# A decoder layer on one core: the last two output-projection pairs, two norms and the first feed-forward round by token halves, in one list schedule

## The reference

```
h = hybrid_mixer(rmsnorm(x, mix_pre_norm[i]), ...)      # ends with: mixed @ w_out, 2048 -> 1024
x = x + rmsnorm(h, mix_post_norm[i])
h = swiglu(rmsnorm(x, ffn2_pre_norm[i]), ffn2_w_gate[i], ffn2_w_up[i], ffn2_w_down[i])
...
def rmsnorm(x, g):
    y = xf * lax.rsqrt(jnp.mean(xf * xf, axis=-1, keepdims=True) + NORM_EPS)
    return (y * g.astype(jnp.float32)).astype(x.dtype)
def swiglu(x, w_gate, w_up, w_down):
    return (jax.nn.silu(x @ w_gate) * (x @ w_up)) @ w_down
```

## Time and profile before

| | |
|---|---|
| median of 3 runs | 2328.41 us (2323.27 to 2330.6) |
| the profiled execution | 2320.75 us, span of its trace 2319.1 us |
| TensorE busy | 2232.7 us, 96% of the span |
| VectorE busy | 1748.3 us, 75% |
| ScalarE busy | 858.4 us, 37% |
| share of TensorE in the chain that ended last | 88% |

### The profile page before, as it was taken

How to read it: one execution, slowest core, us unless ns; L and a number is a source line. 1 busy time by engine, 2 the same in 40 slices (tenths; PEclk the granted TensorE clock), 3 DMA queues, 4 the chain that set the end, 5 groups by cost and what they waited for, 6 DMA issues and landing times.

```text
span 2319.1 us, 29269 instructions
## 1 busy us (share of the span) xinstructions
PE 2232.7 (96%) x10358; PEld 1824.7 (79%) x10358; DVE 1748.3 (75%) x2661; ACT 858.4 (37%) x1357; POOL 206.3 (9%) x181
## 2 busy tenths in 40 slices
PE   7999999999999989999999998998999999999996
PEld 6888888888878767778787677786888888888885
DVE  7877777777768888887776976878787777777766
ACT  6322222222344556665532644214522222222222
POOL 0000000000000333432100316100000000000000
PEclk9999999999999999999999999998999999999998
DMA  4111111111332001002031224114111111111123
GB/s 158 50 55 46 50 54 54 54 54 54 118 111 91 10 19 37 28 28 73 12 108 46 91 91 172 54 43 176 37 64 46 54 54 54 54 54 54 46 100 109
DMA packets 52041, 154.62 MB, mean 67 GB/s; under 512 B 5872, under 2 KB 7920, under 8 KB 49776
## 3 DMA queue, kind: packets, MB, share of 16 engines
q1 hardware_dynamic: 51952, 153.46, 19.5%
HBM read 132.14 MB, written 21.30 MB: 66 GB/s over the span
## 4 chain that ended last, share of the span: by engine, by line
PE 88%; DVE 7%; ACT 2%; issue 2%; DMA 1%; SPq 0%; DVEq 0%; ACTq 0%
PE psum L456 10%; PE psum L455 10%; PE psum L454 10%; PE psum L593 8%; PE psum L594 8%; PE psum L595 8%; PE psum L1640 3%; PE psum L1642 3%; PE psum L1641 3%; PE psum L1786 2%; PE psum L541 1%; PE psum L543 1%; PE psum L542 1%; PE psum L1797 1%; PE psum L1163 1%
## 5 line engine op out<-in xcount | busy, mean ns | idle before, releaser
L1009 DVE TENSOR_TENSOR acc<-psum,acc 128x512 f32<-128x512 f32 x288 | 197.9, 691 | 160.9 <-PE psum L595 158.1
L593 PE MATMUL psum<-act_hi,tile_hi 128*128 128x512 f32 x672 | 261.5, 389 | 0.0
L594 PE MATMUL psum<-act_lo,tile_hi 128*128 128x512 f32 x672 | 261.4, 389 | 0.0
L595 PE MATMUL psum<-act_hi,tile_lo 128*128 128x512 f32 x672 | 261.4, 389 | 0.0
L708 ACT CAST t_hi<-t_raw 128x512 fp32r<-128x512 f32 x144 | 89.6, 622 | 309.9 <-DVE t_raw L869 296.5
L593 PEld LDWEIGHTS psum<-act_hi,tile_hi 128*128 128x128 f32 x672 | 126.1, 188 | 26.2
L595 PEld LDWEIGHTS psum<-act_hi,tile_lo 128*128 128x128 f32 x672 | 126.1, 188 | 26.2
L594 PEld LDWEIGHTS psum<-act_lo,tile_hi 128*128 128x128 f32 x672 | 126.1, 188 | 26.1
L730 ACT ACTIVATE sum<-sum 128x512 f32<-128x512 f32 x72 | 45.6, 633 | 247.6 <-DVE sum L963 152.8
L1640 PE MATMUL psum<-norm_hi,tile_hi 128*128 128x512 f32 x320 | 129.7, 405 | 6.2 <-DVE z_scaled L2047 4.3
L1956 DVE TENSOR_TENSOR probs_t_lo<-psum,probs_t_hi 128x512 fp32r<-128x512 f32 x144 | 96.6, 686 | 47.7 <-ACT probs_t_hi L1874 47.2
(11 more groups left out here) (377 smaller groups left out, 5618.4 us busy)
## 6 DMA issues: line engine op xcount, KB each, us to landing
tile_lo_raw<-in_d SPq DMA_DIRECT2D x40, 512.0 KB, 4.3
gate_raw<-in_gu SPq DMA_DIRECT2D x36, 512.0 KB, 3.8
up_raw<-in_gu SPq DMA_DIRECT2D x72, 256.0 KB, 3.6
raw_tile<-in_w_att SPq DMA_DIRECT2D x28, 512.0 KB, 3.6
gate_up_lo_raw<-in_gu SPq DMA_DIRECT2D x8, 1024.0 KB, 5.2
cum_rows<-cum_scratch SPq DMA_DIRECT2D x8, 1024.0 KB, 4.5
raw_tile<-in_w_out SPq DMA_DIRECT2D x16, 512.0 KB, 3.6
acc<-in_x SPq DMA_DIRECT2D x8, 512.0 KB, 10.7
```

Source lines behind the costliest of these rows:

```text
L593: pe.matmul(o, w_h[:, s, d, :], a_h[:, s, x], start=(s == 0), stop=False)
L594: pe.matmul(o, w_h[:, s, d, :], a_l[:, s, x], start=False, stop=False)
L595: mm = pe.matmul(o, w_l[:, s, d, :], a_h[:, s, x], start=False, stop=(s == 1))
L1009: v.tensor_tensor(x, banks(4 + d % 4), x, ALU.add).then_inc(sem(p + "_acc"), 1)
```

## The change

The last two pairs of the output projection (6 and 7), the post norm of the mixer, the pre norm of the second feed-forward block and that block's first round with its down projection leave their written order and become steps of one plan (`turn_plan`), at the same half-width steps as `t1` and `t3`, and `t2` becomes a half-turn.

- The outputs come in another order: half 0 of pair 6, half 0 of pair 7, then half 1 of both (`OUT_ORDER`). TensorE has outputs, rounds and down outputs in one line "main".
- The post norm is done for each half by itself, and so is the pre norm. The square sums of the pre norm are groups of 4 columns, 16 of them (`cols_of`), in bank 5.
- Scale, residual, high part, square and low part work on half tiles: 16 of each instead of 8. The residual comes in as 16 loads of a half tile, 8 for each half, each into its own place; 16 stores instead of 8.
- In the first round half 0 of both weight tiles comes first (`round 0` is units 0 and 1, 12 matmuls a tile), then half 1 of the first, then half 1 of the second. The down projection's outputs go to other banks (`TURN_DOWN`).
- Pair 7's second weight tile has a raw buffer of its own. The gate/up weights are loaded when pair 7's operands are made, the down weights after the last output. The odd pairs' buffers, the even pairs' weights, the first pair's, and the squares' move to other addresses.
- Ahead of the plan, `out_pe`, `out_act` and `out_dve` end with pair 5, pair 6's operands still made within pair 5. Behind it nothing changes.

The diff, cut to its core. The placing of the buffers:

```diff
         wl = at("tile_lo", 164, [P, 2, KT, P], FR)
-        xs = at("x_stream", 172, [P, 2, S])
+        x_half = [at("x_first_half", 206.75, [P, KT, HALF]), at("x_second_half", 96, [P, KT, HALF])]
+        sq_half = [at("x_squares", 196, [P, 4, HALF]), at("x_squares_next", 172, [P, 4, HALF])]
         sq = at("squares", 180, [P, 2, S])
-        diag = at("rstd_diagonal", 180, [P, CH, P])
-        sqa = at("result_squares", 172, [P, 4, HALF])
+        diag = {"t": at("rstd_diagonal", 180, [P, CH, P]), "g": at("gate_diagonal", 56, [P, CH, P])}
+        sqa = at("result_squares", 112, [P, 4, HALF])
+        raww_last = at("raw_tile_last", 120, [P, KT, P])
         gul_raw = at("gate_up_lo_raw", 136, [P, 2, 2, KT, P])
         wl_raw = at("tile_lo_raw", 164, [P, 2, KT, P])
...
-        out_first = (at("tile_hi_first", 172, [P, 2, KT, P], FR), at("tile_lo_first", 180, [P, 2, KT, P], FR), acth, actl)
-        out_slots = [(wh, wl, acth, actl),
-                     (at("tile_hi_odd", 14, [P, 2, KT, P], FR), at("tile_lo_odd", 22, [P, 2, KT, P], FR),
-                      at("act_hi_odd", 30, [P, 2, S], FR), at("act_lo_odd", 38, [P, 2, S], FR))]
+        out_first = (at("tile_hi_first", 196, [P, 2, KT, P], FR), at("tile_lo_first", 206.75, [P, 2, KT, P], FR), acth, actl)
+        out_slots = [(at("tile_hi_even", 14, [P, 2, KT, P], FR), at("tile_lo_even", 22, [P, 2, KT, P], FR), acth, actl),
+                     (wh, wl, at("act_hi_odd", 172, [P, 2, S], FR), at("act_lo_odd", 180, [P, 2, S], FR))]
 
         psum = ctx.enter_context(nc.psum_tensor("psum", [P, 8, 512], F32))
 
```

The plan, without the sums for the seven-product loop (`planned_sum`, `operand_sum` and their casts, ranks 6 and 7):

```diff
+        OUT_PAIRS = MIX_T // 2
+        OUT_ORDER = [(i, h, d) for h in range(NH2) for i in (OUT_PAIRS - 2, OUT_PAIRS - 1) for d in range(KT)]
+        OUT_DONE = 16 * (OUT_PAIRS - 2)
+        FREE = OUT_DONE + OUT_ORDER.index((OUT_PAIRS - 2, 1, KT - 1)) + 1
+        TURN_BANKS = (0, 2, 6, 0)
+        TURN_DOWN = (4, 5, 2, 3), (4, 5, 6, 7)
+
+        def turn_plan():
+            plan = Plan()
+            add = plan.add
+            last = OUT_PAIRS - 1
+            for n in (2 * last, 2 * last + 1):
+                add("SP", "out_w", ("out_w_in", n), 0.0)
+                add("ACT", "out_w", ("out_w_hi", n), 1.05, ("out_w_in", n))
+                add("DVE", "out_w", ("out_w_lo", n), 1.22, ("out_w_hi", n))
+                add("ACT", "out_w", ("out_a_hi", n), 1.05)
+                add("DVE", "out_w", ("out_a_lo", n), 1.22, ("out_a_hi", n))
+            ready = [("out_w_lo", 2 * last + 1), ("out_a_lo", 2 * last + 1)]
+            for n, u in enumerate(OUT_ORDER):
+                add("PE", "main", ("out", *u), 1.36, ("out_acc", *OUT_ORDER[n - 4]) if n > 3 else None,
+                    *(ready if u[0] == last else ()))
+                add("DVE", "out_acc", ("out_acc", *u), 0.69, ("out", *u))
+            free = ("out", last - 1, 1, KT - 1)
+            whole = ("out_acc", *OUT_ORDER[-1])
+            rings = [(h, d) for h in range(NH2) for d in range(1, KT)]
+            for h in range(NH2):
+                for d in range(KT):
+                    r = rings.index((h, d)) if d else 0
+                    add("ACT", "a_sq", ("a_sq", "t2", h, d), 0.63, ("out_acc", last, h, d),
+                        ("a_sum", "t2", *rings[r - 4]) if r > 3 else None)
+                    if d:
+                        add("DVE", "a_sum", ("a_sum", "t2", h, d), 0.69, ("a_sq", "t2", h, d),
+                            ("a_sum", "t2", h, d - 1) if d > 1 else ("a_sq", "t2", h, 0))
+                rstd_steps(add, f"t2_post{h}", ("a_sum", "t2", h, KT - 1))
+            for n in range(2):
+                add("SP", "gu_in", ("gu_in", n), 6.0, ready[1])
+                add("ACT", "gu", ("gu_hi", n), 2.0, ("gu_in", n))
+                add("DVE", "gu", ("gu_lo", n), 2.3, ("gu_hi", n))
+            for s in range(2):
+                add("SP", "d_in", ("d_in", s), 4.0, ("out", *OUT_ORDER[-1]))
+                add("ACT", "d", ("d_hi", s), 1.05, ("d_in", s))
+                add("DVE", "d", ("d_lo", s), 1.22, ("d_hi", s))
+            for h in range(NH2):
+                for k in range(KT):
+                    add("SP", "x_in", ("x_in", "t2", h, k), 3.0, free if h else None)
+                    add("DVE", "scale", ("scale", "t2", h, k), 0.69, ("rb", f"t2_post{h}"))
+                    add("DVE", "resid", ("resid", "t2", h, k), 0.69, ("scale", "t2", h, k), ("x_in", "t2", h, k))
+                    add("SP", "x_out", ("x_out", "t2", h, k), 3.0, ("resid", "t2", h, k))
+                    add("ACT", "hi", ("hi", "t2", h, k), 0.63, ("resid", "t2", h, k), free if k > 2 else None)
+                    add("DVE", "lo", ("lo", "t2", h, k), 0.69, ("hi", "t2", h, k))
+                    add("ACT", "sq", ("sq", "t2", h, k), 0.63, ("resid", "t2", h, k), ("cols_of", h, k - 4) if k > 3 else None)
+                    add("PE", "cols_of", ("cols_of", h, k), 0.85, ("sq", "t2", h, k),
+                        (("rms", "t2_pre0") if h else whole) if k == 0 else None)
+                e = f"t2_pre{h}"
+                add("ACT", "rstd", ("rms", e), 0.3, ("cols_of", h, KT - 1))
+                add("DVE", "rstd", ("rc", e), 0.9, ("rms", e))
+                add("PE", "rstd", ("rows", e), 1.0, ("rc", e))
+                add("ACT", "rstd", ("rb", e), 0.63, ("rows", e))
+            begin = {0: [("gu_lo", 1), ("rb", "t2_post0")], 2: [("rb", "t2_post1"), whole], 3: [("gate", 0), ("up", 0)]}
+            for v in (0, 2, 3):
+                for k in range(KT):
+                    add("PE", "main", ("round", v, k), 1.36 if v else 2.72, ("lo", "t2", v // 2, k), *(begin[v] if k == 0 else ()))
+            for v in range(4):
+                done = ("round", v if v > 1 else 0, KT - 1)
+                add("DVE", "gate", ("gate", v), 0.69, done, ("silu", v - 1) if v else None, ("rb", f"t2_pre{v // 2}"))
+                add("ACT", "silu", ("silu", v), 0.63, ("gate", v), ("prod", v - 1) if v else None)
+                add("DVE", "up", ("up", v), 0.69, done, ("act_lo", v - 1) if v else None, ("rb", f"t2_pre{v // 2}"))
+                add("DVE", "prod", ("prod", v), 0.69, ("silu", v), ("up", v))
+                add("ACT", "act_hi", ("act_hi", v), 0.58, ("prod", v), ("resid", "t2", 1, KT - 1))
+                add("DVE", "act_lo", ("act_lo", v), 0.69, ("act_hi", v))
+            for h in range(NH2):
+                for d in range(KT):
+                    add("PE", "main", ("down", h, d), 1.36, ("act_lo", 2 * h + 1), ("d_lo", 1),
+                        ("rb", "t2_pre1"), ("down_copy", (8 * h + d - 4) // 8, (d - 4) % 8) if 8 * h + d > 3 else None)
+                    add("DVE", "down_copy", ("down_copy", h, d), 0.69, ("down", h, d), ("planned_sum", 16), ("x_out", "t2", 1, KT - 1))
...
+            rank = dict(RSTD_RANK)
+            rank |= {("DVE", "out_acc"): 1, ("DVE", "a_sum"): 2, ("DVE", "lo"): 2, ("DVE", "resid"): 3, ("DVE", "scale"): 4,
+                     ("ACT", "a_sq"): 1, ("ACT", "hi"): 2, ("ACT", "sq"): 3, ("DVE", "out_w"): 0, ("ACT", "out_w"): 0,
+                     ("PE", "main"): 1, ("PE", "cols_of"): 0, ("DVE", "gate"): 1, ("DVE", "up"): 1, ("DVE", "prod"): 1, ("DVE", "act_lo"): 1,
+                     ("DVE", "down_copy"): 1, ("ACT", "silu"): 1, ("ACT", "act_hi"): 1, ("ACT", "d"): 6, ("ACT", "s"): 6,
+                     ("ACT", "t_hi"): 7, ("DVE", "sums"): 6, ("DVE", "t_sum"): 6, ("DVE", "t_lo"): 7}
+            return plan.order(rank)
+
+        TURN = turn_plan()
+
+        TURN_RSTD = {"t2_post0": (3, 2), "t2_post1": (7, 6), "t2_pre0": (5, 4), "t2_pre1": (5, 4)}
+
```

TensorE's steps and SyncE's; the steps of ScalarE and VectorE hold the same instructions as before at half width, with the waits that the plan lists:

```diff
+            def round_step(v, k):
+                if k == 0 and v == 0:
+                    wait(pe, p + "_gu_lo", 2)
+                    pe.wait_ge(sem("rstd_rb"), RSTD["t2_post0"])
+                elif k == 0 and v == 2:
+                    pe.wait_ge(sem("rstd_rb"), RSTD["t2_post1"])
+                elif k == 0:
+                    wait(pe, p + "_gate", 1)
+                    wait(pe, p + "_up", 1)
+                h = v // 2
+                pe.wait_ge(sem("half_lo"), past_half("t2", h, KT) + k + 1)
+                for u in (0, 1) if v == 0 else (v,):
+                    for m in range(2):
+                        mm = pair(TURN_BANKS[u] + m, u % 2, m, k, h)
+                if k == KT - 1:
+                    mm.then_inc(sem(p + "_gu_mm"), 2 if v == 0 else 1)
+
...
+        def turn_pe(pe, step, e):
+            if step == "out":
+                i, h, d = e
+                n = OUT_DONE + OUT_ORDER.index((i, h, d))
+                w_h, w_l, a_h, a_l = out_slot(i)
+                wait(pe, "wo_d_lo", 2 * i + 2)
+                wait(pe, "wo_act_lo", 2 * i + 2)
+                wait(pe, "wo_acc", n - 3)
+                o, x = banks(4 + d % 4), half(h)
+                for s in range(2):
+                    pe.matmul(o, w_h[:, s, d, :], a_h[:, s, x], start=(s == 0), stop=False)
+                    pe.matmul(o, w_h[:, s, d, :], a_l[:, s, x], start=False, stop=False)
```

(32 more changed lines are left out.)

550 lines of the change are left out of this document (347 added, 203 removed).

## The result

The kernel after takes 2310.03 us (median; 2306.84 to 2316.57 over 4 runs), the kernel before 2327.64 us beside it (2323.27 to 2330.6 over 4 runs). The ratio is 0.9933, 95% interval 0.9914 to 0.9952: faster by 0.67%, 15.6 us (the medians themselves are 17.6 apart). The forecast was 2315.9, a gain of 12.5.

The account below looks back on a forecast made before the run. TensorE was taken as the bound; the 146.7 us stretch becomes 130.0 of work plus 4.2 of waits. The gain, 13.5 + 4.4 - 1.1 - 0.1 - 4.2 = 12.5, gives 2315.9 us; range 2312.9 to 2318.9, over all cases 2310 to 2325.

Parts of the forecast that it names:

- TensorE sets the end, time won ahead of the loop arrives whole: Whole kernel: TensorE, busy 96% of the span, bounds it; time won before the steady loop at 1690.1 us arrives whole.
- Removed 17.2 - 3.7 = 13.5: Post norm after the last output: of a 17.2 us gap only 3.7 us of TensorE helper matmuls stay, saving 13.5.
- Price of the order 1.2: Pair 6's outputs: pair 7's operands, needed earlier, delay accumulations; TensorE stalls 1.2 us, bounds 0 and 3.
- Square sums 16 x 0.98, rows 1.8: Pre norm: 16 column groups at 0.98 us, 15.7 against 14.6; rows as two half ones, 1.8 against 1.7.
- Waits in a list order 4.2: Changed stretch: TensorE idles 4.2 us, as in the earlier half-turn, the 1.2 us stall included; bounds 1.2 and 9.
- Slow clock 4.4 taken as gone: Changed stretch: 3.6 us of slow-clock matmuls and 0.8 us unexplained disappear; bounds -4.4 to 0.
- VectorE 118 to 121: Changed stretch: VectorE's busy time rises from 116.6 us to 118 to 121 with more, half-width instructions.
- The half-0 root within 6 us of half 1: Post norm, a sign to show in the profile: the half-0 root comes within 6 us after half 1 begins.
- Granted clock 1.0 in all of it: From pair 6's first matmul to the loop, a sign to show: TensorE's granted clock is 1.0 throughout.
- rival 2: Round 0 of half 0 at the low clock: 19.2 us lost, time 2335.1; chance with any other loss 0.07.
- doesn't do what it says: Plan places half-0 root and rows late on TensorE's queue: gain only 1.5 us, time 2327; chance 0.11.
- Rival 1: VectorE becomes the bound over the changed stretch, taking 139 us: gain 7.7, time 2320.7; chance 0.16.

Follow-up runs that it names:

- the repeats: The kernel after, unchanged, profiled and timed twice more: 2311.41 us (ratio to before 0.9941) and 2311.98 us (0.9941).
- copies early: Against fp32r columns: VectorE's first down-product copies wait for the 13th operand sum instead of the 17th; 2312.48 us, ratio to before 0.9931.
- norm held: Against after: the half-0 post norm's column matmuls and all behind them planned after the last output; 2319.65 us, ratio to before 0.9974.
- pair order: Against after: outputs in the old order, both halves of pair 6, then both of pair 7; 2313.31 us, ratio to before 0.9953.
- sums first: Against after: pair 7's low parts ranked below the accumulations on VectorE; 2309.17 us, ratio to before 0.9928.
- ScalarE's copies with fp32 columns: Against copies on ScalarE: the pre norm's column sums back to after's one-column fp32 matmuls; 2311.81 us, ratio to before 0.9944.
- fp32r columns: Against sums first: pre-norm column sums in fp32r with two moving columns instead of fp32 with one; 2309.03 us, ratio to before 0.9941.
- copies on ScalarE: Against copies early: the sixteen down-product copies on ScalarE instead of VectorE; 2304.17 us, ratio to before 0.9911.

## Why the prediction was right, step by step

- *TensorE sets the end, time won ahead of the loop arrives whole*: right. The stretch lost 14.9 us by one profile and 13.4 and 14.9 by the repeats; the ratios, 0.9933 and 0.9941, are 14 to 16 us. From the loop's first matmul to the end of the span the profile of before took 629.0 us and the three of after 629.3 to 629.6; all other kernels lie between 628.9 and 630.3, but copies early (632.3), whose loop began with 12 slow matmuls.
- *Removed 17.2 - 3.7 = 13.5*: right in mechanism, shown by the held norm. The helpers that stayed are the two column blocks at 0.8 us and two row matmuls at 0.45 us, each with some more in the matmul behind it, 0.1 us for a column block and 0.41 for a row matmul: 0.45 + 0.41 = 0.86 for the rows, as written.
- *Price of the order 1.2*: 1.12, released by the accumulation, at the fifth output as said. VectorE's timeline shows the four low parts ahead of the accumulations; with the ranks turned it is gone.

```profile
1554.73 1.23 DVE L2629 TENSOR_TENSOR tile_lo<-raw_tile,tile_hi 128x1024 fp32r<-128x1024 f32 x1 [0.45 <-ACT tile_hi L2624]
1555.88 1.22 DVE L2649 TENSOR_TENSOR act_lo_odd<-y_features,act_hi_odd 128x1024 fp32r<-128x1024 f32 x1
1557.01 1.22 DVE L2629 TENSOR_TENSOR tile_lo<-raw_tile_last,tile_hi 128x1024 fp32r<-128x1024 f32 x1
1558.15 1.22 DVE L2649 TENSOR_TENSOR act_lo_odd<-y_features,act_hi_odd 128x1024 fp32r<-128x1024 f32 x1
1559.28 3.19 DVE L1598 TENSOR_TENSOR acc<-psum,acc 128x512 f32<-128x512 f32 x5
```

- *Square sums 16 x 0.98, rows 1.8*: all helpers together, with what the matmul behind each loses at full clock, take about 19.6 us, where 21.2 was written; a column group is nearer 0.9, since up to three run in one block. 1.6 us too much.
- *Waits in a list order 4.2*: mis-sized. They are 1.1, 3.1 us less. The half-turn behind the first block was the nearest row; why it waits more than this one was not looked into.
- *Slow clock 4.4 taken as gone*: mis-sized, though inside its own bounds (-4.4 to 0), and the reason given for it did not hold. Most of the low clock stood behind column groups that the plan had put together again into one block of up to 2.85 us, not "under 1 us". "Granted clock 1.0 in all of it" fell: 7 matmuls at 0.43 (1.5 us) in after and in its second repeat, 17 (3.5 us) in its first. With the two terms above, 134.2 - 1.6 - 3.1 + 1.5 = 131.0; the last 0.8 us of the 131.8 are matmuls a few hundredths further apart than the pitch. That the sum comes within 2.4 us of the stretch is in part luck: two terms were too dear, one too cheap.
- *VectorE 118 to 121*: 119.1.
- *The half-0 root within 6 us of half 1*: 6.4. No harm came of it.
- *2315.9*: 5.9 us too slow, outside the likeliest case's own range (2312.9 to 2318.9) and inside the whole one (2310 to 2325) by 0.03 us only, which is luck with a scatter of some 3 us in the medians; the repeats, 2311.4 and 2312.0, are 4 us below it. By the ratio the gain was 3.1 us larger than forecast, 2.4 of it in the stretch (134.2 against 131.8); the other 2.8 are the scatter of medians, 0.8 that of before's (2328.41 and then 2327.64).
- *Rivals.* Slower at the low clock (2) and "doesn't do what it says" (3) fell; but the sign that was to show rival 2, matmuls of 0.43 us in the first round, did appear: 7 to 17 of them, one or two short pieces, far from the 63 that would have decided it. The stretch from 1611.34 to 1637.03 that the prediction set against this rival has no idle in it, so it cannot tell what short idle spells do. Rival 1 (VectorE the bound) fell for this kernel, where VectorE managed 119.1 of 131.8 us, 90% instead of 87, and TensorE waits for it once. It holds right behind: with 6 to 11 us of TensorE's work gone, VectorE ends last, and its place is where the down products begin, which the prediction had not named.

## What to carry over

Here two engines were busy for 99% and 90% of a stretch, and one relieved alone showed nothing; in such a case take the work off both in one kernel before you call either edit worthless. A wait for an engine that moves down its list when a dependency is loosened, and keeps its size, points to that engine's load and asks for another engine, not another order. Price the low clock as a term of its own wherever one-column fp32 matmuls or stalls remain, and do not take the zero end of its range as the likely value.

## What the runs showed of the hardware

**The clock can fall behind a block of one-column fp32 matmuls, with no idle at all.** In after, TensorE had been busy without a break since 1560; twelve large matmuls, a block of 24 column records of 2.85 us, and then 0.43 us a matmul for 3 us:

```profile
1631.66 0.39 PE L490 MATMUL psum<-norm_hi,gate_up_lo 128*128 128x512 f32 x1
1631.89 2.85 PE L1533 MATMUL psum<-ones,x_squares_next 128*128 128x1 f32 x24
1634.60 0.77 PE L488 MATMUL psum<-norm_hi,gate_up_hi 128*128 128x512 f32 x1
1635.17 0.63 PE L489 MATMUL psum<-norm_lo,gate_up_hi 128*128 128x512 f32 x1
...
1637.99 0.39 PE L490 MATMUL psum<-norm_hi,gate_up_lo 128*128 128x512 f32 x1
```

Behind the block just before it, of the same 24 records, it did not:

```profile
1626.46 2.73 PE L1533 MATMUL psum<-ones,x_squares_next 128*128 128x1 f32 x24
1629.05 0.48 PE L488 MATMUL psum<-norm_hi,gate_up_hi 128*128 128x512 f32 x1
1629.37 0.39 PE L489 MATMUL psum<-norm_lo,gate_up_hi 128*128 128x512 f32 x1
```

The seven profiles with this plan and fp32 columns (after and its two repeats, pair order, norm held, sums first, and ScalarE's copies with fp32 columns) have 14 such blocks of 24 records. Behind 8 of them 7 to 12 large matmuls ran at 0.43 us, behind 6 none. In all three profiles of after it is the second of two such blocks, 12 large matmuls apart; what decides it is not shown. Smaller blocks were followed by a fall only where a wait of 0.3 us or more had come shortly before, but for one place in the first repeat: 16 records, a row matmul and 8 records without a break, then 8 matmuls at 0.43. Where fp32r took the columns and no long wait was left, in one profile, no run of matmuls was at the low level. The engine's busy share does not show this, the granted clock of a 15-us piece does (0.89 above). The Trainium skill (TensorE: Matmul & The Clock Gate, "A second HAM failure mode: psum-queue depth-cycling") ties such swings to short idle spells between groups of matmuls; here some falls came behind waits of 0.3 us and more, which agrees, and some without any idle, which that section does not tell of.

**Long waits.** A 6.5 us wait was followed by 9 matmuls at the low level, a 9.7 us one by 7 and by 9, a 5.9 us one by 12: 1.4 to 2.4 us on top of each wait. The waits of 0.5 and 1.5 us at the loop's first matmul were followed by none. A 0.8 us wait ahead of the post norm's fp32 columns was followed by 6 in fp32r columns, by 12 in copies early and by none in copies on ScalarE, with the same instructions around it.

**A reciprocal on VectorE is long**: 3.35 us for 512 against 0.69 for a product of 512, and 0.18 for four.

**VectorE beside GpSimd.** In the mixer, ahead of the change, a subtraction of 1.22 us took 3.31 us in after while GpSimd ran a product of 2.41 on `y_features`:

```profile
1440.38 3.31 DVE L2629 TENSOR_TENSOR tile_lo_even<-raw_tile,tile_hi_even 128x1024 fp32r<-128x1024 f32 x1
```

```profile
1440.20 2.41 POOL L2768 TENSOR_TENSOR y_features<-y_features,z_in 128x1024 f32<-128x1024 f32 x1
```

The Trainium skill (SBUF — State Buffer, "SBUF: two separate sides") says of the pair of ports which the two share that it is held for a whole instruction and the other blocks; 0.18 + 3.31 less 2.41 leaves 1.08 for the subtraction itself behind the end of the product, about its 1.22, so these rows agree with it.
